# Second expert stage: the third prefetched expert moves behind two narrow ones, and loads take buffers as they come free

## The reference, cut to what matters

```python
# 256 tokens, 16 experts, the best 2 experts of each token's group
for e in range(16):
    hid = silu(t @ w_gate[e]) * (t @ w_up[e])     # 1024 -> 512
    out = out + combine[:, e:e+1] * (hid @ w_down[e])   # 512 -> 1024
```

## Time and profile before

| | value |
|---|---|
| median of 3 runs | 1451.58 us |
| the profiled execution's own time | 1454.33 us |
| its span in the trace | 1452.5 us |
| TensorE busy | 1394.9 us, 96% |
| bytes moved by DMA | 423.05 MB |
| VectorE / ScalarE busy | 42% / 15% |

### The profile page before, as it was taken

The page is one execution under the profiler, slowest core; times in us unless marked ns, Lnnn a source line. Parts: engine busy times, 40 slices in busy tenths (PEclk is TensorE's granted clock), DMA queues, the critical chain, the costliest instruction groups (busy, mean ns, idle before and its releaser), DMA issues.

```text
span 1452.5 us, 21416 instructions
## 1 busy us (share of the span) xinstructions
PE 1394.9 (96%) x9210; PEld 983.7 (68%) x9210; DVE 607.4 (42%) x1249; ACT 220.3 (15%) x430; POOL 18.0 (1%) x44
## 2 busy tenths in 40 slices
PE   9999999999999999999999999898998998999976
PEld 7888888678888886555445444444687887565543
DVE  1557998989982334222221111122412426122112
ACT  0220100421112013110111010011211203211001
POOL 0000000000000000001000000000010000000000
PEclk9999999999999999999999999999999999999999
DMA  9731222964434686999999999999473557799995
GB/s 381 315 138 58 72 117 80 355 231 175 174 130 160 267 346 267 363 424 428 406 427 426 425 428 428 425 426 409 118 243 115 212 219 276 296 385 423 425 425 235
DMA packets 36343, 423.05 MB, mean 291 GB/s; under 512 B 4353, under 2 KB 5769, under 8 KB 10777
## 3 DMA queue, kind: packets, MB, share of 16 engines
q1 hardware_dynamic: 33408, 415.33, 69.9%
q0 software_dynamic: 1664, 4.52, 0.9%
q10 hardware_dynamic: 1176, 1.84, 0.8%
HBM read 419.05 MB, written 2.62 MB: 290 GB/s over the span
## 4 chain that ended last, share of the span: by engine, by line
PE 74%; DMA 20%; DVE 3%; issue 1%; ACT 0%; POOL 0%; SPq 0%; DVEq 0%; ACTq 0%; POOLq 0%
PE PP L968 18%; PE PP L1318 13%; PE PP L1355 7%; PE MB L1098 7%; DMA ZC<-in_w_moe 6%; DMA KQ<-in_w_moe 5%; PE MB L1293 4%; PE PP L1122 3%; PE MB L1096 3%; DMA relb_d<-small 3%; PE PP L1006 3%; DMA RA<-in_w_moe 2%; DMA ring<-in_w_moe 2%; PE PP L1038 2%; PE PP L1327 2%; PE PP L1285 1%
## 5 line engine op out<-in xcount | busy, mean ns | idle before, releaser
L968 PE MATMUL PP<-uT,ring 128*128 128x256 f32 x704 | 155.3, 383 | 0.0
L968 PEld LDWEIGHTS PP<-uT,ring 128*128 128x128 f32 x704 | 135.0, 192 | 19.1 <-issue 0.5
L2173 DVE TENSOR_SCALAR wctx<-wctx 128x1 f32<-128x1 f32 x46 | 7.1, 154 | 278.5 <-PE PP L1318 230.7
L1655 DVE SCALAR_TENSOR_TENSOR ZC<-ZC,vec 128x256 f32<-128x256 f32 x240 | 116.2, 484 | 7.8
L1318 PE MATMUL PP<-ring,const 128*64 128x256 f32 x800 | 91.0, 380 | 5.5 <-DMA ring<-in_w_moe 4.5
L1293 PE MATMUL MB<-V 64*128 64x512 f32 x336 | 93.5, 638 | 1.7 <-DVE V L2206 0.9
L1318 PEld LDWEIGHTS PP<-ring,const 128*64 128x64 f32 x800 | 58.2, 137 | 40.7 <-issue 8.3
L2192 DVE SCALAR_TENSOR_TENSOR V<-V,wctx 128x256 f32<-128x256 f32 x84 | 40.7, 485 | 99.2 <-PE MB L1293 79.0
L800 ACT ACTIVATE V<-PP 128x256 f32<-128x256 f32 x42 | 16.1, 384 | 318.5 <-PE PP L1318 303.6
L1355 PE MATMUL PP<-ring,const 128*64 128x512 f32 x272 | 62.1, 598 | 0.6 <-ACT const L817 0.6
L968 PE MATMUL PP<-Vc,ring 128*128 128x256 f32 x256 | 55.7, 379 | 0.0
(11 more groups left out here) (542 smaller groups left out, 2103.4 us busy)
## 6 DMA issues: line engine op xcount, KB each, us to landing
ring<-in_w_moe SPq DMA_DIRECT2D x51, 2048.0 KB, 26.2
RA<-in_w_moe SPq DMA_DIRECT2D x18, 2048.0 KB, 24.4
ZC<-in_w_moe SPq DMA_DIRECT2D x18, 2048.0 KB, 25.5
Vc<-in_w_moe SPq DMA_DIRECT2D x17, 2048.0 KB, 25.0
KQ<-in_w_moe SPq DMA_DIRECT2D x17, 2048.0 KB, 26.0
extra<-in_w_moe SPq DMA_DIRECT2D x17, 1792.0 KB, 23.6
ring<-in_w_ada SPq DMA_DIRECT2D x12, 2048.0 KB, 10.6
ring<-in_w_gates SPq DMA_DIRECT2D x7, 2048.0 KB, 8.0
```

Source lines behind the costliest of these rows:

```text
L968: ins = pe.matmul(out[:, c, :], W[:, k * width + at:k * width + at + P], X[:, k, :], start=k == 0, stop=k == K - 1)
L1655: ins = V_.scalar_tensor_tensor(conv[:, t, :], zpad[:, t, k:k + L], tap, conv[:, t, :], ALU.mult, ALU.add)
```

## The change

- `FIXED` becomes the steps (0, 1, 4). The plan is now: 0 M, 1 M, 2 N, 3 N, 4 MN (expert 2), 5 N, 6 N, 7 MN, 8 to 11 M, 12 and 13 N, 14 M. `SORTED` are the other twelve steps, with the same ranks in the same order.
- The list of loads of the second stage is no longer in the order of the steps: first the nine loads of steps 0, 1 and 4, then those of steps 2, 3, 5, 6, 7 and so on. Jobs keep the order of the steps.
- Buffers of the second stage are dealt out by which of the nine comes free first; the ninth stays in use to the end. `TAILS` is not edited.
- VectorE writes the tables of ids and offsets in pieces, since fixed and sorted steps no longer lie side by side.

```diff
-FIXED, LAST_RANK = 3, 12
+FIXED, LAST_RANK = (0, 1, 4), 12
@@ plan
-        kinds = ["M", "M", "MN"] + ["MN" if r == 0 else "M" if r <= 5 else "N" for r in RANK_OF]
+        kinds = ["MN" if r == 0 else "M" if r <= 5 else "N" for r in RANK_OF]
+        for step, kind in zip(FIXED, ("M", "M", "MN")):
+            kinds.insert(step, kind)
+SORTED = [step for step in range(EXPERTS[1] - 1) if step not in FIXED]
@@ make_jobs
+    arrive = list(FIXED) + SORTED
+    coming = [3 * step + q for step in arrive for q in range(3)]
-        if phase in ("moe0", "moe1"):
+        if phase == "moe1":
+            if n >= BAYS:
+                first = min(range(len(at_work)), key=lambda x: at_work[x][0])
+                at_work.append((coming[n], at_work.pop(first)[1]))
+                return at_work[-1][1]
+            bay = SPARE if n == BAYS - 1 else ROUNDS[phase][n]
+            at_work.append((coming[n], bay))
+            return bay
+        if phase == "moe0":
@@ sort_experts
-                    V_.tensor_copy(tab[0:1, 40 + FIXED:40 + E - 1], o_("ids")[0:1, 0:R - 1])
+                    for nth, step, count in runs(SORTED):
+                        V_.tensor_copy(tab[0:1, 40 + step:40 + step + count], o_("ids")[0:1, nth:nth + count])
@@ route
-                    V_.tensor_copy(tab[0:1, 0:E], o_("offs")[0:1])
+                    for nth, step, count in runs(list(FIXED) + SORTED + [E - 1]):
+                        V_.tensor_copy(tab[0:1, step:step + count], o_("offs")[0:1, nth:nth + count])
-                    V_.tensor_scalar(tab[0:1, 32:32 + 8], o_("offs")[0:1, 0:8], float(SLOTS), 512.0, ALU.add, ALU.min)
+                    for nth, step in enumerate(list(FIXED) + SORTED):
+                        if len(PLANS[1][step]) == 2:
+                            V_.tensor_scalar(tab[0:1, 32 + step:33 + step], o_("offs")[0:1, nth:nth + 1], float(SLOTS), 512.0, ALU.add, ALU.min)
```

More of the change, by code:

```diff
@@ L77, with runs @@
 WINDOWS = [sum(len(x) for x in steps) for steps in PLANS]
+SORTED = [step for step in range(EXPERTS[1] - 1) if step not in FIXED]
+def runs(steps):
+    out = []
+    for nth, step in enumerate(steps):
+        if out and out[-1][1] + out[-1][2] == step:
+            out[-1][2] += 1
+        else:
+            out.append([nth, step, 1])
+    return out
 def scattered_with(n, w):
@@ L111 @@
                     ("dneg", 512), ("ln2", 512), ("nfb", 512), ("mctx", 4), ("causal", 128), ("tri", 128), ("pcol", 1),
-                    ("slot", 130), ("eps", 2), ("fixed", 2 * FIXED),
+                    ("slot", 130), ("eps", 2), ("fixed", 2 * len(FIXED)),
                     ("step_rank", 13), ("step_base", 13), ("step_cap", 13))
@@ L127, in make_jobs @@
 def make_jobs():
-    jobs, loads, dense = [], [], 0
+    jobs, loads, dense, at_work = [], [], 0, []
+    arrive = list(FIXED) + SORTED
+    coming = [3 * step + q for step in arrive for q in range(3)]
     at = dict.fromkeys(ROUNDS, 0)
@@ L144, in experts @@
     def experts(n):
-        for e in range(EXPERTS[n] - 1):
+        steps, first = arrive if n else range(EXPERTS[0] - 1), len(loads)
+        for step in steps:
             for q in range(3):
-                jobs.append(dict(src=f"moe{n}", b=3 * e + q, kind="moe", half=0, w=len(loads), i=len(jobs)))
-                loads.append(dict(src=f"moe{n}", b=3 * e + q, bay=bay_of(f"moe{n}")))
+                loads.append(dict(src=f"moe{n}", b=3 * step + q, bay=bay_of(f"moe{n}")))
+        for step in range(EXPERTS[n] - 1):
+            for q in range(3):
+                jobs.append(dict(src=f"moe{n}", b=3 * step + q, kind="moe", half=0, w=first + 3 * steps.index(step) + q, i=len(jobs)))
     order = (("mix1", (("ada", 4, ["ada"]), ("piece", PIECES, []), ("glu", 4, ["cm8"]), ("q", 2, ["cm8"]),
@@ L497, in load @@
                 block = s[x["b"]]
-                if x["src"] == "moe1" and x["b"] >= 3 * FIXED:
-                    step = x["b"] // 3
+                step = x["b"] // 3
+                if x["src"] == "moe1" and step in FIXED:
+                    block = s[3 * FIXED.index(step) + x["b"] % 3]
+                elif x["src"] == "moe1":
                     if x["b"] % 3 == 0:
-                        if step == FIXED:
+                        if step == SORTED[0]:
                             sp.wait_ge(moe[1]["items_ready"], 2)
@@ L2053, in assigned_rows @@
                     V_.tensor_tensor(G[:, c], Ek[:, 0:2], Ek[:, 2:4], ALU.add).then_inc(m["g_ready"], 1)
-                R = E - FIXED
+                F = len(FIXED)
+                R = E - F
                 along = lambda x: x.unsqueeze(1).to_broadcast([P, R, R])
@@ L2059, in sort_experts @@
                 def sort_experts():
-                    link(V_.scalar_tensor_tensor(o_("key"), r_("cnt")[:, FIXED:E], float(E), iota[:, 0:R], ALU.mult, ALU.subtract))
+                    link(V_.scalar_tensor_tensor(o_("key"), r_("cnt")[:, F:E], float(E), iota[:, 0:R], ALU.mult, ALU.subtract))
                     link(V_.tensor_tensor(order_of, along(o_("key")), across(o_("key")), ALU.is_gt))
@@ L2064, in sort_experts @@
                     link(V_.tensor_tensor(order_of, along(o_("rank")), across(cst("step_rank", R)), ALU.is_equal))
-                    link(V_.tensor_tensor(order_by, order_of, along(iota[:, FIXED:E]), ALU.mult))
+                    link(V_.tensor_tensor(order_by, order_of, along(iota[:, F:E]), ALU.mult))
                     link(V_.tensor_reduce(o_("ids"), order_by, AX.X, ALU.add))
-                    V_.tensor_copy(tab[0:1, 40 + FIXED:40 + E - 1], o_("ids")[0:1, 0:R - 1])
+                    for nth, step, count in runs(SORTED):
+                        V_.tensor_copy(tab[0:1, 40 + step:40 + step + count], o_("ids")[0:1, nth:nth + count])
                     V_.tensor_copy(tab[0:1, 72:73], o_("ids")[0:1, R - 1:R]).then_inc(m["items_ready"], 1)
                 def sorted_places():
-                    link(V_.tensor_tensor(order_by, order_of, along(e_("off")[:, FIXED:E]), ALU.mult))
-                    V_.tensor_copy(o_("offs")[:, 0:FIXED], e_("off")[:, 0:FIXED])
-                    link(V_.tensor_reduce(o_("offs")[:, FIXED:E], order_by, AX.X, ALU.add))
+                    link(V_.tensor_tensor(order_by, order_of, along(e_("off")[:, F:E]), ALU.mult))
+                    V_.tensor_copy(o_("offs")[:, 0:F], e_("off")[:, 0:F])
+                    link(V_.tensor_reduce(o_("offs")[:, F:E], order_by, AX.X, ALU.add))
                     by_expert = order_of.rearrange("p s e -> p e s")
@@ L2077, in sorted_places @@
                         link(V_.tensor_tensor(order_by, by_expert, along(cst(of, R)), ALU.mult))
-                        V_.tensor_copy(o_(name)[:, 0:FIXED], cst("fixed", 2 * FIXED)[:, nth * FIXED:(nth + 1) * FIXED])
-                        link(V_.tensor_reduce(o_(name)[:, FIXED:E], order_by, AX.X, ALU.add))
+                        V_.tensor_copy(o_(name)[:, 0:F], cst("fixed", 2 * F)[:, nth * F:(nth + 1) * F])
+                        link(V_.tensor_reduce(o_(name)[:, F:E], order_by, AX.X, ALU.add))
                 assigned_rows(0)
@@ L2435, in constants @@
     caps = [capacity(x) for x in steps] + [SLOTS]
-    put("fixed", np.broadcast_to(np.array(base[:FIXED] + caps[:FIXED]), (P, 2 * FIXED)))
+    put("fixed", np.broadcast_to(np.array([x[step] for x in (base, caps) for step in FIXED]), (P, 2 * len(FIXED))))
     put("step_rank", np.broadcast_to(np.array(RANK_OF + (LAST_RANK,)), (P, 13)))
-    put("step_base", np.broadcast_to(np.array(base[FIXED:]), (P, 13)))
-    put("step_cap", np.broadcast_to(np.array(caps[FIXED:]), (P, 13)))
+    put("step_base", np.broadcast_to(np.array([base[step] for step in SORTED] + base[-1:]), (P, 13)))
+    put("step_cap", np.broadcast_to(np.array([caps[step] for step in SORTED] + caps[-1:]), (P, 13)))
     return c
```

## The result

The changed kernel takes 1456.47 us (median of 20 runs, 1452.86 to 1458.34) against 1451.66 for the kernel before in the same sessions: ratio 1.0033, 95% interval 1.0025 to 1.0041, which is 4.8 us slower (3.6 to 6.0). Forecast were 3.9 us slower and 1455.5.

What follows compares the result with a forecast made beforehand. The weight stream was taken to bound the second expert stage. Its 4.7 us gain is lost to the tail's late loads: tail's gate +3.2, tail itself +0.7, so +3.9 on 1451.58 gives 1455.5 us; range 1452.0 to 1459.5.

Steps and rivals of the forecast that it cites:

- The bound: Second expert stage: the weight stream sets the end, full from 1287.3 on; what is lost before is never made good.
- Part 1: Narrow steps first free buffers early, so loads 15 to 17 go out earlier; the stream gains 5.1 us by load 17.
- the term of 4.7: Weight stream's gain in us left after VectorE's extra table writing; step 14 then ends at 1421.4.
- Part 2: Five more small VectorE copies ahead of the first hidden values, exposed: load 11 and all behind come 0.4 us later.
- Part 3: Tail's loads wait for the down of step 14; tail's gate at 1430.0, 3.2 us later than before.
- The tail itself: From the tail's gate to the end of its down: 15.3 us with half clock, 0.7 more than before.
- The sum: Tail's gate +3.2 and tail itself +0.7, output as before: +3.9 us, 1455.5.
- A: Rival, within 0.2%: stream gain 5.3, no VectorE cost, clock kept, the down's load is the bound: +1.6 us; chance 0.24.
- B: Rival, faster: tail's loads issued ahead of step 14 after all, gaining 4.7 us, 1446.9; chance 0.09.
- C: Rival, slower by far: half clock through gate, up and most of the rest of the tail: +8.0 us, 1459.6; chance 0.07.
- D: Rival: step 2 waits for its loads and the stream gains nothing, 1460.2 us; chance 0.03.

Runs made afterwards that it cites:

- e1: Changed kernel with the second stage's tail buffers named (6, 1, 2) instead of (3, 6, 1): 1447.11 us, ratio 0.9966.
- e7: Changed kernel with tail buffers (6, 1, 2) and FIXED = (0, 1, 3), one narrow step ahead of the wide one: 1446.65 us, ratio 0.9968.
- e8: Changed kernel with tail buffers (6, 1, 2) and FIXED = (0, 1, 5), three narrow steps ahead of the wide one: 1447.17 us, ratio 0.9969.
- e10: Changed kernel with tail buffers (6, 1, 2) and 12 small matmuls in TensorE's wait before the second stage's first transpose: 1448.72 us, ratio 0.9972.
- e3: Changed kernel with FIXED = (0, 1, 2), so the old order of steps with the new dealing of buffers: 1452.86 us, ratio 1.0001.
- e9: Changed kernel with 30 small matmuls after the down of step 14, in the wait ahead of the tail's gate: 1455.70 us, ratio 1.0030.
- e12: Changed kernel with 36 small matmuls after the down of step 14, in the wait ahead of the tail's gate: 1457.77 us, ratio 1.0052.
- e2: Kernel before with one wait added, so the tail's loads are issued only after the down of step 14: 1460.44 us, ratio 1.0051.
- e4: Changed kernel with the old round of buffers, so only the order of steps is new: 1465.87 us, ratio 1.0083.
- e5: Changed kernel with 64 small matmuls after the down of step 14, ahead of the tail's gate: 1461.99 us, ratio 1.0078.
- e6: Changed kernel with tail buffers (6, 1, 2) and 15 linked two-element copies added to VectorE's table writing: 1452.02 us, ratio 1.0000.
- e11: Kernel before with 15 linked two-element copies added to VectorE's table writing: 1455.39 us, ratio 1.0025.

## Why the prediction was right, and where its terms were not

- **The bound.** Right. Three groups lie apart by when the stream becomes full and whether the tail's loads follow it without a gap: both good (e1, e7, e8, e10: ratios 0.9966 to 0.9972), the old stream (before, e3: 1.0000 and 1.0001), and a late tail or a late stream (changed, e9, e12, e2, e4: 1.0030 to 1.0083). Left out are the runs in which added work delays the path (e5, e6, e11). Within a group the profiles don't predict the time: e10 has the earlier stream and not the shorter time.
- **Part 1, loads 15 to 17 issued early.** Right in the mechanism: they go out 21.5, 22.7 and 26.9 us after load 11's issue in the changed kernel (1239.47), against 24.9, 29.9 and 37.9 in the kernel before. e3 and e4 show that it takes order and dealing together. TensorE kept up: no wait for DMA at steps 2 and 3.
- **The size of part 1.** "Load 17 at 1282.2" came true (1266.37 + 15.9 = 1282.3), by luck: the stage began 3.1 us earlier in this execution, and loads 11 to 14 came later within it. After S, load 17 is 1.9 us earlier than before, not 4.7, and load 44 2.3. The step that failed is "until then steps 0 and 1 and the issue of loads 9 to 14 are the same". Load 11 is issued 2.4 later after S, because behind TensorE's wait for the first hidden values the granted clock was 0.76 over 14 us (first row of the windows above): e4 has the same wait (3.49 against 3.48) with the clock at 1.00, and issues load 11 at 36.3 instead of 38.9, as does e10, in which the clock was kept. Where the clock stayed up with the new order (e8, e9, e10), load 17 lands at S + 79.2 to 79.7, 3.9 to 4.4 earlier than before, and 3.3 to 4.0 earlier than in e2 and e3: there the term of 4.7 was nearly right.
- **Part 2, table writing.** Right in its place and about in size: the first transpose waits 3.48 in the changed kernel, 3.20 and 3.25 in e2 and e3, which is 0.25 against 0.4. The 1.82 of the earlier trace rows, from which I took the exposure, is no price of the VectorE work; e2, which has the same tables, has 3.20. The difference is TensorE's clock in front of the wait. In the traced execution of before it was 0.50 for 6.8 us, so TensorE came later to the wait, while the transpose behind it started at S + 28.7 (28.2 in e2, 28.5 in the changed kernel). Windows at about S + 7 to S + 14, in this order of before, e2, the changed kernel and e9 (columns as in rows 3):

```profile
1210.60:1217.40 6.80, 6.80 (x32) 6.55 (x32) 4.99 (x17) 1.11 (x3) 0.00 (x0) 0.50 0.98 409
1206.80:1213.60 6.80, 5.54 (x48) 5.34 (x49) 5.51 (x20) 2.21 (x7) 0.00 (x0) 1.00 1.00 419
1207.50:1214.30 6.80, 5.53 (x49) 5.34 (x49) 5.48 (x21) 2.24 (x7) 0.00 (x0) 1.00 1.00 416
1207.70:1214.50 6.80, 5.71 (x27) 5.42 (x27) 6.32 (x21) 1.14 (x4) 0.00 (x0) 0.50 0.97 391
```

e8 (wait 2.09) and e9 (1.00) have the early fall too. That added work there is exposed is shown by e6 and e11.

- **Part 3, the tail's prefetch.** Right in the mechanism and its own durations: bay 3 for load 44, the wait ended by the down of step 14, 1.0 us to the issue (1421.64 against 1420.65), 7.5 to land, a wait of 8.57 where 8.6 was said. e1 and e2 show it from both sides. The points in time came out well for the same lucky reason as load 17: step 14 was forecast to end at 1421.4 and ended at 1420.65, but after S it ends only 2.3 earlier than before (220.1 against 222.4), and the tail's gate begins 5.6 later than before (228.7 against 223.1), not 3.2.
- **The tail itself.** I added 1.9 for the half clock and took off 1.2 for the wait at the up. The clock did fall, and the gate took 5.31. But the tail took 1444.06 - 1429.23 = 14.83, 0.2 more than before and not 0.7: gate and up are bound by the landing of the up load, and half clock fills time that was waiting before. (Without the half clock the prediction's sum would be 15.3 - 13.4 = 1.9 less by its own terms, and not the 1.5 that it states.)
- **The sum.** By the terms as measured after S: stream -2.3 at load 44, wait +7.9, tail +0.2, which is +5.8 as the last down (243.5 - 237.7) in the two profiled executions; the medians of 20 runs give +4.8. No run accounts for the 1.0 between them. The forecast of +3.9 had the stream 2.4 too good and the tail 0.5 too dear.
- **Rivals.** A (within 0.2%) needed the clock kept and a gain of 5.3; the interval (3.6 to 6.0) excludes it. Its account of the tail was the better one, though: the down starts when its load has landed (1440.41 against 1440.1). B (tail's loads ahead of step 14) is what e1 makes of the kernel: forecast 1446.9, measured 1447.11. C (half clock through all of the tail) did not come: the up already runs at 3.62. D (waits for loads at step 2) did not come.
- **Left open.** Whether the change itself brings about the clock fall behind the wait for the first hidden values. It is there in six of the ten executions with the new order and the new tables (changed, e1, e5, e6, e7, e12; of the other four e10 has the clock keeper in that wait) and in none of the four with the old order (before, e2, e3, e11); but e4 has the wait (3.49 us) with the clock at 1.00, and so has e11 (3.59), so that the wait's length alone doesn't decide it. It also differs between executions of the same instructions: the changed kernel, e5, e9 and e12 are one program up to the tail, and in e9 the clock fell at about S + 9 and not behind the wait. One profiled execution of each kernel can't tell how often either happens, so how much of the 20 timed runs' 4.8 us goes back to it stays open.

## What to carry to other kernels

When buffers are dealt anew, look at every list that names buffers by number: here three numbers decided between 4.8 us slower and 4.9 us faster, and the loss could be read off before by asking which job the first load behind the loop waits for. A stream that is full to the end gains only by beginning to be full earlier; a shorter step in front that frees buffers does that, but only if the next loads are given those buffers. Compare stages from an event in front of them that the change doesn't touch, since a number that fits in absolute time may fit by luck.

## What was not expected of the hardware

- The tail's first load landed 7.5 us after its issue in the changed kernel and in e2 with TensorE idle, 8.6, 8.6 and 8.7 in e5, e9 and e12, where TensorE was running small matmuls, while the third landed 17.4 after its issue in all five. Why was not tried.
- With 2.75 us of idle time behind 6.96 us of matmuls the granted clock still fell (e9: gate 5.28 us), and with 1.47 us behind 8.30 it did not (e12: 3.67).
- The same wait can leave the clock as it is or not: ahead of the gate of step 14 TensorE waited 3.12 us in e1 and 3.05 in e10; the first 28 matmuls behind it took 3.24 us in e1 and 4.93 in e10.
- A 128x128x128 fp32 matmul of the clock keeper costs 0.2275 us, as two records.
